# Gaps in front of four groups of SBUF buffers, so that the operands of the split products start at one address modulo 512 bytes

## The chip, the cores and the metric

One core of a Trainium2 chip runs the whole program in one launch. The metric is device time in microseconds (us), the median of several executions.

## The reference

512 tokens of width 1024 pass through two blocks in float32. The first has two layers, each a mix of two attentions, a mixture of experts and a gated embedding. The second has one layer: windowed attention, a linear recurrence, block attention, and a dense gated feed-forward. Cut to its matrix products:

```python
def first_block(x, ...):
    for i in range(2):
        u = rmsnorm(x, g_mix[i]) @ w_in[i]
        y_a = stick_breaking_attention(...) @ w_br_a[i]
        y_b = differential_attention(...) @ w_br_b[i]
        merged = sigmoid(gate_a) * y_a + sigmoid(gate_b) * y_b
        x = x + merged @ w_o[i]
        x = x + hierarchical_moe(rmsnorm(x, g_ffn[i]), ...)
        x = x + (p[i] @ w_ple[i]) * sigmoid(rmsnorm(x, g_ple[i]) @ w_ple_gate[i])
    return rmsnorm(x, g_final)

def hybrid_layer(x, ...):
    z = rms_norm(x, g_mix) @ w_in
    merged = gt[:, :, 0] * (o_a @ p_a) + gt[:, :, 1] * (o_b @ p_b) + gt[:, :, 2] * (o_c @ p_c)
    x = x + merged @ w_out
    gate, up = jnp.split(rms_norm(x, g_ffn) @ w_gu, 2, axis=-1)
    return x + (jax.nn.silu(gate) * up) @ w_down
```

## The kernel before, in words

All activations stay in SBUF, tokens or features on the 128 partitions. Nearly every dense product is a **split product** (`split_product`, line 134, its matmul is line 137): both operands are held as a high and a low part of type float32r, and three matmuls add high x high, high x low and low x high into one PSUM bank:

```python
for n, (left, right) in enumerate(((a[0], b[0]), (a[0], b[1]), (a[1], b[0]))):
    last = nc.tensor.matmul(out, left, right, start=(start and n == 0), stop=(stop and n == 2), ...)
```

`left` is the stationary operand, 128 columns that TensorE loads first; `right` is the moving one, 512 columns. The profile names them in the order moving, stationary: `banks<-h_split,w_high` moves h_split over w_high.

Weights come through a `Stream` (line 143): SyncE issues the load of a 512 KB piece into one of four raw buffers, GpSimd casts it to the high part (line 178), VectorE subtracts for the low part (line 189), and TensorE uses one of three split buffers. `columns` (line 195) moves the 512 tokens of the normalised activations `h_split` over a weight chunk, eight chunks of three matmuls for a piece; `rows` moves weights over tokens. `Merge` (line 1179) computes for each of eight output chunks the branch products (`ya`, `yb`, in the second block also `yc`, moving, over the stream's weights) and the gates (`columns`, two per chunk in the first block, done early inside the attention for three of the eight chunks; three per chunk in the second). `Product` (line 1290) moves weights over `op_split`, the split form of the merged activations: 24 matmuls for each of eight chunks, and for each of 22 hidden chunks in the second block's down product. The gate product of the embedding has its own stream, `pg`. In the attentions, `columns` and `rows` of later pieces stand between the attention's own matmuls.

The order of the work is written out by hand for each engine (the `sync`, `gpsimd`, `tensor`, `scalar` and `vector` functions), with semaphores between them.

**Where buffers lie.** Memory is a stack in each partition: a buffer starts where the last one ended, rounded up to 32 bytes. `region` (with `h_split` over its first part) is placed by `Core`. The first block's large buffers share one space, the ring, that begins at `ring_base` (in `program`): the stream `w1`, `ya_transposed`, `yb_transposed`, `op_split` are placed in it by `Opening`, as are later `expert_ring`, `ex_xs`, `ex_xsT` and `pg_high`. Expert weights take six slots in turn, four in the ring and two in the region. The second block's stream `w2` begins where `first_stack` began, and `yb2_transposed`, `yc2_transposed` and `op2_split` follow the window attention's buffers. Both blocks' buffers appear in the profile without the block's number (`w_high`, `yb_transposed`, `op_split`).

Of the kernel before, what the change touches and what calls it, by code (L numbers as in the profile page):

```python
# [21 lines left out]
F32 = mybir.dt.float32  # L22
# [7 lines left out]
P = 128  # L30
# [6 lines left out]
NEG = -1e30  # L37
HD = 64
SCALE = HD ** -0.5


class Core:


    def __init__(self, nc, ctx):
        def sb(name, shape, dt=F32):
            return ctx.enter_context(nc.sbuf_tensor(name, shape, dt))

        self.nc = nc
        self.used_sems = set()  # L50
        self.ps = ctx.enter_context(nc.psum_tensor("banks", [P, 8, 512], F32))
        self.x = sb("x_tokens", [P, NT, D])
        self.ident = sb("identity", [P, P])
        self.ident_r = sb("identity_r", [P, P], F32R)
        self.neg_tri = sb("neg_tri", [P, P], F32R)
        self.neg_ones = sb("neg_ones", [P, P], F32R)
        self.neg_before = sb("neg_before", [P, P], F32R)
        self.strict_bias = sb("strict_bias", [P, P], F32R)
        self.chunk_bias = sb("chunk_bias", [P, P], F32R)
        self.rope_swap = sb("rope_swap", [P, P])  # L60
        self.shift = sb("shift", [P, 16])
        self.halves = sb("halves", [P, 2, 2, NT])
        self.norm_ss, self.norm_g = sb("norm_ss", [P, 2, NT]), sb("norm_g", [P, 2, DC])
        self.layer = ""
        offset = nc.sbuf_base
        assert offset % 32 == 0
        self.region = sb("region", [P, 3 * NT * D])
        self.h = nc.alloc_sbuf_tensor_at("h_split", [P, 2, DC, S], F32R, offset=offset)
        self.spare = self.region[:, 2 * NT * D:]
        self.spare_tiles = self.spare.rearrange("p (t d) -> p t d", t=NT)  # L70

    def room(self, ctx, name, shape, dt=F32):
        return ctx.enter_context(self.nc.sbuf_tensor(name + self.layer, shape, dt))
# [152 lines left out]
def row_piece(w, c, chunks, off, cols):  # L226

    return [(chunks, cols, rows_pc(w)[:, c:c + chunks, off:off + cols])]
# [291 lines left out]
def stick_breaking(k, ctx, room, norm, st, yT, da_raw):  # L520
# [114 lines left out]
    def scalar(act):  # L635
        def take_q(i, bank):
            pair = (i - SB_COLUMNS) // 2
            act.wait_ge(st.used, i + 1)
            dst = qT[:, pair % 2, :] if pair < pairs else da_raw[:, 0, :]
            nc.scalar.activation(dst, k.ps[:, bank, :], ACT.Copy, scale=SCALE).then_inc(q_ready, 1)  # L640

# [191 lines left out]
def differential(k, ctx, room, st, lams, gain, lam_init, keep, cosT, sinT, raw, yT, early, line_store=None):  # L833
# [139 lines left out]
    def scalar(act):  # L973
        def take_raw(head, n, bank):
            act.wait_ge(st.used, columns_of(head, n) + 1)
            nc.scalar.activation(raw[:, n, :], k.ps[:, bank, :], ACT.Copy,
                                 scale=1.0 if n else SCALE).then_inc(sem["raw_ready"], 1)

# [1112 lines left out]
def window_attention(k, ctx, room, norm, st, bias, first_bias, yT, conv, rooms_free):  # L2091
# [172 lines left out]
    def scalar(act):  # L2264
        def take_q(i, bank):
# [3 lines left out]
            if g:  # L2269
                src, dst = src.rearrange("p (i r) -> p r i", r=APART), dst.rearrange("p (r i) -> p r i", r=APART)  # L2270
            nc.scalar.activation(dst, src, ACT.Copy, scale=SCALE).then_inc(q_ready, 1)

# [199 lines left out]
def block_attention(k, st, lines, bias, first_bias, yT, opened):  # L2472
# [11 lines left out]
    with ExitStack() as ctx:  # L2484
# [90 lines left out]
        def _(act):  # L2575
# [14 lines left out]
            def take_q(i):  # L2590
                act.wait_ge(st.used, i + 1)
                nc.scalar.activation(qT[:, (i - QK) // 2 % 2, :], k.ps[:, 7, :], ACT.Copy, scale=SCALE).then_inc(q_ready, 1)

# [473 lines left out]
def second_layer(k, t, lines, out, ple_of, ending, ring_base):  # L3067
    nc = k.nc
    ended = set(k.used_sems)
    w_in = t["w_in_2"][0]  # L3070
    width = WINDOW_HEADS * HD
    window = len(WINDOW_GROUPS) * width
    lru, block = 3 * window, 3 * window + 1024
    gates = block + 1536
    packs = (0, 1), (2,)
    with ExitStack() as mix:
        st = Stream(k, mix, "w2", [row_piece(w_in, 4 * e, 4, 2 * window, width) for e in (0, 1)]
                    + [column_piece(w_in, 2 * window + g * width + pair * P) for g in (1, 2) for pair in (0, 1)]
                    + [column_piece(w_in, kind * window + g * width + pair * P) for pair in (0, 1)
                       for g in range(len(WINDOW_GROUPS)) for kind in (0, 1)]  # L3080
                    + [column_piece(w_in, lru + c * P) for c in range(8)]
                    + [row_piece(w_in, 2 * e, 2, block + 1024, 512) for e in range(4)]
                    + [column_piece(w_in, block + kind * 512 + pair * P) for pair in range(4) for kind in (0, 1)]
                    + merge_pieces(w_in, (gates, gates + D, gates + 2 * D), (t["p_a_2"][0], t["p_b_2"][0], t["p_c_2"][0]),
                                   packs)
                    + [[(1, D, t["w_out_2"][0][c * P:(c + 1) * P, :].rearrange("p (a n) -> p a n", a=1))] for c in range(DC)]
                    + [column_piece(t["w_gu_2"][0], part * FFN + f * P) for f in range(FC) for part in (0, 1)]
                    + [[(1, D, t["w_down_2"][0][f * P:(f + 1) * P, :].rearrange("p (a n) -> p a n", a=1))] for f in range(FC)])
        mix_base = nc.sbuf_base
        yaT = mix.enter_context(nc.sbuf_tensor("ya2_transposed", [P, 2, 2, S], F32R))  # L3090
        bias = mix.enter_context(nc.sbuf_tensor("biases", [P, 4, S], F32))
        conv = Convolution(k, mix, t["conv_w_2"][0], t["conv_b_2"][0], t["lru_ba_2"][0], t["lru_bx_2"][0], t["lru_lam_2"][0])
        window_bias_loads, block_bias_loads = window_bias(k, mix, bias, lines), block_bias(k, mix, bias, lines)
        with ExitStack() as room:
            junk = nc.alloc_sbuf_tensor_at("fn_junk", [P, NT * D], F32, offset=ring_base + 4 * 18432)[:]
            closing_g = nc.alloc_sbuf_tensor_at("fn_g", [P, D], F32, offset=ring_base + 4 * 26624)[:]
            sig = nc.alloc_sbuf_tensor_at("pe_sig", [P, 4, 512], F32, offset=ring_base + 4 * 27648)[:]
            xn = nc.alloc_sbuf_tensor_at("mix2_xn", [P, NT, D], F32, offset=ring_base + 4 * 22528)[:]
            norm = FinalNorm(k, mix, "mix2", t["g_mix_2"][0], (6, 7), xn, junk, t["g_final"], k.spare_tiles, closing_g)
            moe, ple, gate_stream = ple_of(mix, norm, sig, junk, st)  # L3100
            attention = window_attention(k, mix, room, norm, st, bias, window_bias_loads, yaT, conv, (gate_stream.used, 2 * NT))

            def sync(sp):
                norm.load_closing(sp)
                ple[0](sp)

            border(k, moe, (sync, *ple[1:]), attention)
        ending.close()
        ybT = mix.enter_context(nc.sbuf_tensor("yb2_transposed", [P, 2, 4, S], F32R))
        qkv_base = nc.sbuf_base  # L3110
        block_qkv = mix.enter_context(nc.sbuf_tensor("ba_qkv", [P, 8, S], F32))
        opened = (block_qkv[:, 0:2, :], block_qkv[:, 2:4, :], block_qkv[:, 4:8, :])
        recurrence(k, st, (18, 26, 30), conv, t["lru_wa_2"][0], t["lru_wx_2"][0], ybT, block_bias_loads, opened, ended)
        k.used_sems -= ended


        assert S // 256 - 1 <= 3
        ycT = mix.enter_context(nc.sbuf_tensor("yc2_transposed", [P, 2, 4, S], F32R))
        block_attention(k, st, lines, bias, block_bias_loads, ycT, opened)
        mergedT = k.spare.rearrange("p (c s) -> p c s", c=DC)  # L3120
        split = nc.alloc_sbuf_tensor_at("op2_split", [P, 2, 2, S], F32R, offset=qkv_base)
        silu = nc.alloc_sbuf_tensor_at("ff_silu", [P, 2, S], F32, offset=qkv_base + 4 * 4 * S)
        final_g = nc.alloc_sbuf_tensor_at("final_g", [P, D], F32, offset=qkv_base + 4 * 6 * S)
        hiddenT = nc.alloc_sbuf_tensor_at("ff_hiddenT", [P, FC, S], F32, offset=mix_base)
        assert mix_base + 4 * FC * S <= qkv_base
        sig, part = (mix.enter_context(nc.sbuf_tensor("mg2_" + n, [P, 2, S], F32)) for n in ("sig", "part"))
        m = Merge(k, mix, "mg2", st, 38, packs, ((yaT, 2), (ybT, 4), (ycT, 4)), mergedT, sig, part)
        op = Product(k, mix, "op2", st, m.end, DC, mergedT, split)
        fd = Product(k, mix, "fd", st, m.end + DC + 2 * FC, FC, hiddenT, split)
        second_half(k, st, m, op, fd, t["g_ffn_2"][0], t["g_final_2"], hiddenT, silu, final_g, out)  # L3130
# [39 lines left out]
def first_layer(k, t, i, ctx, ending, r, ring_base, scratch, o, line_store):  # L3170


    nc = k.nc
# [12 lines left out]
            line_store)  # L3186
    o.branches.close()
    k.used_sems -= ended
    assert -(-nc.sbuf_base // 32) * 32 == ring_base
    mergedT = k.spare.rearrange("p (c s) -> p c s", c=DC)  # L3190
    m = Merge(k, ctx, "mg", st, MERGE_PIECES, o.packs, ((o.yaT, 4), (o.ybT, 4)), mergedT, o.sig, o.part,
              (0, 1, 2, 3, 4, 7, 5, 6), early, early_ready)
# [41 lines left out]
def program(nc, t, out):  # L3234
    with ExitStack() as ctx:
        k = Core(nc, ctx)
# [4 lines left out]
        first_stack = ctx.enter_context(ExitStack())  # L3241
# [6 lines left out]
        xn_rows = nc.dram_tensor("xn_rows", [S, D], F32)  # L3248
        y_rows = nc.dram_tensor("y_rows", [2 * S, D], F32)
        r = Routing(nc, first_stack)  # L3250
        ring_base = -(-nc.sbuf_base // 32) * 32
        ple = None
        layers = [ctx.enter_context(ExitStack()) for _ in range(DEPTH)]
        endings = [ctx.enter_context(ExitStack()) for _ in range(DEPTH)]
# [111 lines left out]
```

## Time and profile before

| | us |
|---|---|
| median of three runs | 2525.43 |
| the three runs | 2525.5, 2521.73, 2525.43 |
| span of the profiled execution, first to last instruction | 2525.1 |
| TensorE busy (11776 matmuls) | 2315.6 |
| VectorE, ScalarE, GpSimd busy | 1001.0, 585.6, 410.2 |

No own device time stands beside the profiled execution other than its span; the median of the runs is 0.3 above it. In the profile TensorE's matmuls are pipelined: each is shown with a duration of about 390 ns, while the next begins after some 230 ns. So what a matmul takes in a long train is read from the start of one to the start of another, divided by the number between, and not from its duration. A row of the timeline merges neighbours of a kind (x2), and of the three matmuls of a split product the one with the low weights stands alone.

### The profile page before, as it was taken

How to read it: one execution, taken by the hardware profiler on the slowest of the kernel's cores; microseconds unless marked ns; L12 is line 12 of the kernel's file. 1: busy time of each engine (PE TensorE's matmuls, PEld its weight loads, DVE VectorE, ACT ScalarE, POOL GpSimd, SP SyncE). 2: the span in 40 equal slices, each digit the busy share in tenths (PEclk: the TensorE clock that was granted, in tenths of full speed). 3: DMA queues.
4: the chain of work that ended last, by engine and by line, in shares of the span. 5: the costliest groups of instructions: out<-in, count | busy, mean ns of one | idle time of the engine just before them, and what ended most of it. 6: DMA issues, size and time to landing. Idle time of an engine off the chain costs nothing. (4 is left out here: it accounts for less than half of the span.)

```text
span 2525.1 us, 29142 instructions
## 1 busy us (share of the span) xinstructions
PE 2315.6 (92%) x11776; PEld 1707.1 (68%) x11776; DVE 1001.0 (40%) x1730; ACT 585.6 (23%) x1211; POOL 410.2 (16%) x404
## 2 busy tenths in 40 slices
PE   7989999588889999999778988899999999999998
PEld 5766788444447766688644545787767887888886
DVE  5445533511135354543521114545653334322234
ACT  2433401211123352321301113423442001100011
POOL 2011121112211101111111211111111221111111
PEclk9999999799998999999989999899999999999999
DMA  4114535699982212232779995222322333233321
GB/s 147 51 44 102 133 106 203 235 410 415 415 332 67 67 34 61 64 89 89 305 306 416 415 398 190 68 84 68 88 76 71 93 103 101 84 99 94 100 92 67
DMA packets 291540, 402.85 MB, mean 160 GB/s; under 512 B 31306, under 2 KB 230730, under 8 KB 273478
## 3 DMA queue, kind: packets, MB, share of 16 engines
q1 hardware_dynamic: 276444, 373.31, 42.0%
q0 software_dynamic: 10176, 16.81, 1.8%
q10 hardware_dynamic: 4778, 10.76, 1.6%
q8 instruction: 98, 1.61, 0.3%
q14 instruction: 44, 0.36, 0.0%
HBM read 388.99 MB, written 30.15 MB: 166 GB/s over the span
## 5 line engine op out<-in xcount | busy, mean ns | idle before, releaser
L137 PE MATMUL banks<-h_split,w_high 128*128 128x512 f32 x2624 | 829.4, 397 | 2.7 <-PEq L3035 1.7
L137 PEld LDWEIGHTS banks<-h_split,w_high 128*128 128x128 f32 x2624 | 481.5, 188 | 107.9 <-issue 8.2
L189 DVE TENSOR_TENSOR w_low<-w_raw,w_high 128x1024 fp32r<-128x1024 f32 (+1 forms) x264 | 316.9, 1201 | 526.6 <-POOL w_high L178 526.5
L178 POOL CAST w_high<-w_raw 128x1024 fp32r<-128x1024 f32 (+1 forms) x264 | 278.2, 1055 | 1475.1 <-PE banks L137 1352.2
L137 PE MATMUL banks<-h_split,w_low 128*128 128x512 f32 x1312 | 514.6, 392 | 0.0
L137 PEld LDWEIGHTS banks<-h_split,w_low 128*128 128x128 f32 x1312 | 246.5, 188 | 55.0
L137 PE MATMUL banks<-w_high,op_split 128*128 128x512 f32 x736 | 231.3, 394 | 1.0 <-DVE mg_part L1269 1.0
L1839 PE MATMUL banks<-expert_ring,ex_xsT 128*64 128x256 f32 x1472 | 180.2, 400 | 17.3 <-DMA expert_ring<-in_w_exp_up 14.3
L137 PEld LDWEIGHTS banks<-w_high,op_split 128*128 128x128 f32 x736 | 138.2, 188 | 34.0 <-DVE mg_part L1269 2.2
L1839 PEld LDWEIGHTS banks<-expert_ring,ex_xsT 128*64 128x64 f32 x1472 | 107.5, 144 | 75.7 <-DMA expert_ring<-in_w_exp_up 15.5
L137 PE MATMUL banks<-w_low,op_split 128*128 128x512 f32 x368 | 144.7, 393 | 0.0
L1798 POOL DMA_INDIRECT y_rows<-ex_y,route_row x66 | 65.8, 997 | 394.7 <-ACT ex_y L1882 394.7
L1910 DVE TENSOR_TENSOR ex_hid<-ex_silu,banks 128x128 f32<-128x128 f32 x66 | 19.0, 288 | 269.7 <-ACT ex_silu L1887 269.7
L137 PE MATMUL banks<-w_high,h_split 128*128 128x512 f32 (+1 forms) x384 | 121.4, 391 | 2.7 <-DVE h_split L337 2.5
L1253 ACT ACTIVATE mg_sig<-banks 128x512 f32<-128x512 f32 x44 | 26.3, 598 | 347.3 <-PE banks L137 347.3
L1828 PE MATMUL banks<-identity,ex_xs 128*128 128x128 f32 x272 | 44.1, 311 | 64.1 <-DMA ex_xs<-xn_rows,route_token 41.2
L1857 PE MATMUL banks<-expert_ring,ex_hidT 128*64 128x512 f32 x368 | 94.9, 639 | 0.9 <-issue 0.9
L1828 PEld LDWEIGHTS banks<-identity,ex_xs 128*128 128x128 f32 x272 | 36.0, 198 | 78.4 <-DMA ex_xs<-xn_rows,route_token 52.1
L137 PE MATMUL banks<-pg_high,h_split 128*128 128x512 f32 x256 | 86.2, 412 | 2.3 <-issue 2.3
L137 PEld LDWEIGHTS banks<-w_high,h_split 128*128 128x128 f32 x384 | 73.0, 195 | 18.3 <-DVE h_split L337 3.7
L1882 ACT ACTIVATE ex_y<-banks 128x512 f32<-128x512 f32 x66 | 39.4, 598 | 187.7 <-PE banks L1857 187.7
L137 PEld LDWEIGHTS banks<-w_low,op_split 128*128 128x128 f32 x368 | 69.1, 188 | 15.9
(424 smaller groups left out, 2768.6 us busy)
## 6 DMA issues: line engine op xcount, KB each, us to landing
w_raw<-in_w_in SPq DMA_DIRECT2D x142, 512.0 KB, 4.1
expert_ring<-in_w_exp_gate SPq DMA_DIRECT2D x46, 1024.0 KB
expert_ring<-in_w_exp_up SPq DMA_DIRECT2D x46, 1024.0 KB
expert_ring<-in_w_exp_down SPq DMA_DIRECT2D x46, 1024.0 KB
w_raw<-in_w_gu SPq DMA_DIRECT2D x44, 512.0 KB, 4.1
region<-in_w_exp_gate SPq DMA_DIRECT2D x20, 1024.0 KB
region<-in_w_exp_up SPq DMA_DIRECT2D x20, 1024.0 KB
region<-in_w_exp_down SPq DMA_DIRECT2D x20, 1024.0 KB
```

Source lines behind the costliest of these rows:

```text
L137: last = nc.tensor.matmul(out, left, right, start=(start and n == 0), stop=(stop and n == 2), skip_group_check=True)
L178: self.nc.gpsimd.tensor_copy(self.high[:, i % self.SPLIT, 0:n], self.raw[:, i % self.RAW, 0:n]).then_inc(self.high_ready, 1)
L189: self.nc.vector.tensor_tensor(self.low[:, i % self.SPLIT, 0:n], self.raw[:, i % self.RAW, 0:n], self.high[:, i % self.SPLIT, 0:n].bitcast ...
L1253: self.nc.scalar.activation(out, gate, ACT.Sigmoid).then_inc(self.sig_done, 1)
L1798: nc.gpsimd.indirect_dma_start(out=y_halves, in_=y[:, n % Y, :], in_offset=None, out_offset=bass.IndirectOffsetOnAxis(ap=r.row[:, at:at + ...
L1828: last = nc.tensor.transpose(k.ps[:, c // 4, (c % 4) * P:(c % 4 + 1) * P], xs[:, q % X, c::DC], k.ident[:])
L1839: last = nc.tensor.matmul(k.ps[LANES * h:LANES * (h + 1), 2 + side, 0:2 * P].rearrange("p (g n) -> p g n", g=2), xsT[:, q % X, c, LANES * ...
L1857: last = nc.tensor.matmul(k.ps[LANES * h:LANES * (h + 1), 5 + n % 2, :], hidT[:, n % 2, LANES * f:LANES * (f + 1)], slots[n % U][1][:, f, ...
L1882: nc.scalar.activation(y[:, n % Y, :], k.ps[:, 5 + n % 2, :], ACT.Copy).then_inc(sem["y_ready"], 1)
L1910: nc.vector.tensor_tensor(hid[:, n % 2, :], silu[:, n % 2, :], k.ps[:, 2 + n % 2, P:2 * P], ALU.mult).then_inc(sem["hid_ready"], 1)
```

## The change

`aligned` allocates an unused gap such that the next buffer starts at a multiple of 512 bytes. It is called at four places: before `region`, before the ring, before the second block's stream, and before `yb2_transposed`.

```diff
+LINE_BYTES = 512
...
-        offset = nc.sbuf_base
-        assert offset % 32 == 0
+        offset = self.aligned(ctx, "region")
         self.region = sb("region", [P, 3 * NT * D])
...
+    def aligned(self, ctx, name):
+        gap = -(-(-self.nc.sbuf_base // 32) * 32) % LINE_BYTES
+        if gap:
+            ctx.enter_context(self.nc.sbuf_tensor(name + "_gap", [P, gap // 4], F32))
+        assert self.nc.sbuf_base % LINE_BYTES == 0
+        return self.nc.sbuf_base
...
     with ExitStack() as mix:
+        k.aligned(mix, "w2")
         st = Stream(k, mix, "w2", [row_piece(w_in, 4 * e, 4, 2 * window, width) for e in (0, 1)]
...
         ending.close()
+        k.aligned(mix, "yb2")
         ybT = mix.enter_context(nc.sbuf_tensor("yb2_transposed", [P, 2, 4, S], F32R))
...
-    assert -(-nc.sbuf_base // 32) * 32 == ring_base
+    assert nc.sbuf_base == ring_base
...
-        ring_base = -(-nc.sbuf_base // 32) * 32
+        ring_base = k.aligned(first_stack, "ring")
```

The addresses in a partition that the allocation gives, before and after, in bytes, and their rest modulo 512:

| buffer | before | rest | after | rest |
|---|---|---|---|---|
| identity | 32896 | 128 | 32896 | 128 |
| region, h_split | 37216 | 352 | 37376 | 0 |
| route_w_high | 94624 | 416 | 94784 | 64 |
| ring, ya_transposed | 99008 | 192 | 99328 | 0 |
| yb_transposed | 115392 | 192 | 115712 | 0 |
| pg_high | 148160 | 192 | 148480 | 0 |
| da_diff | 156352 | 192 | 156672 | 0 |
| w1_raw | 172736 | 192 | 173056 | 0 |
| w1_high | 189120 | 192 | 189440 | 0 |
| ex_xs | 197312 | 192 | 197632 | 0 |
| op_split | 213696 | 192 | 214016 | 0 |
| w2_raw | 88928 | 352 | 89088 | 0 |
| w2_high | 105312 | 352 | 105472 | 0 |
| ya2_transposed | 129888 | 352 | 130048 | 0 |
| wa_probs | 199808 | 128 | 199968 | 288 |
| yb2_transposed | 162944 | 128 | 163328 | 0 |
| yc2_transposed | 195712 | 128 | 196096 | 0 |
| op2_split | 179328 | 128 | 179712 | 0 |
| ba_probs | 212096 | 128 | 212480 | 0 |

A low part lies a multiple of 4096 bytes behind its high part. The instructions of every engine and their order are the same as before.

## Rows read from the trace of the kernel before

**Rows 1.** The page, busy time of each engine (us, share of the span, instructions)
```profile
PE 2315.6 (92%) x11776; PEld 1707.1 (68%) x11776; DVE 1001.0 (40%) x1730; ACT 585.6 (23%) x1211; POOL 410.2 (16%) x404
```

**Rows 2.** Windows: us from start, length, TensorE busy (matmuls), granted clock, DMA share, GB/s
```profile
25.00:300.00 275.00, 263.30 (x1301) 1.00 0.33 85
325.00:390.00 65.00, 65.00 (x281) 1.00 0.34 103
505.00:720.00 215.00, 188.63 (x1303) 0.96 1.02 413
735.00:800.00 65.00, 60.92 (x237) 0.95 0.38 139
2150.00:2390.00 240.00, 239.03 (x1061) 1.00 0.32 95
```

**Rows 3.** Waits of TensorE: line <- what ended it: us in total, times, longest
```profile
PE banks L1828 <- DMA ex_xs<-xn_rows,route_token: 41.2, 24, 3.4
...
PE banks L1839 <- DMA expert_ring<-in_w_exp_up: 14.3, 6, 3.7
...
PE banks L581 <- issue: 5.0, 6, 0.8
...
PE banks L137 <- DVE h_split L337: 4.5, 5, 1.5
...
PE banks L596 <- DVE sb_stay L721: 3.5, 2, 1.7
```

**Rows 4.** The chain that ended last: start us, us, what
```profile
2154.13 361.26 PE banks L137 x1578
```

**Rows 5.** Timeline of TensorE, feed-forward of the second block: start us, us, instruction
```profile
2200.03 0.39 PE L137 MATMUL banks<-h_split,w_low 128*128 128x512 f32 x1
...
2209.55 0.39 PE L137 MATMUL banks<-h_split,w_low 128*128 128x512 f32 x1
```

**Rows 6.** Timeline of TensorE, merge of the second block
```profile
1926.19 0.61 PE L137 MATMUL banks<-h_split,w_high 128*128 128x512 f32 x2
...
1933.67 0.61 PE L137 MATMUL banks<-ya_transposed,w_high 128*128 128x512 f32 x2
...
1935.03 0.63 PE L137 MATMUL banks<-yb_transposed,w_high 128*128 128x512 f32 x2
...
1939.23 0.63 PE L137 MATMUL banks<-yc_transposed,w_high 128*128 128x512 f32 x2
```

**Rows 7.** Timeline of TensorE, merge of the first layer
```profile
323.81 0.63 PE L137 MATMUL banks<-h_split,w_high 128*128 128x512 f32 x2
...
335.05 0.63 PE L137 MATMUL banks<-ya_transposed,w_high 128*128 128x512 f32 x2
...
337.81 0.61 PE L137 MATMUL banks<-yb_transposed,w_high 128*128 128x512 f32 x2
...
340.53 0.63 PE L137 MATMUL banks<-h_split,w_high 128*128 128x512 f32 x2
```

**Rows 8.** Timeline of TensorE, down product of the second block
```profile
2409.98 0.63 PE L137 MATMUL banks<-w_high,op_split 128*128 128x512 f32 x2
...
2419.78 0.40 PE L137 MATMUL banks<-w_high,op_split 128*128 128x512 f32 x1
```

**Rows 9.** Matmul groups of 25 to 1620 us, then of 1620 to 2525: xcount | busy us, mean ns
```profile
L137 PE MATMUL banks<-h_split,w_high 128*128 128x512 f32 x1024 | 332.8, 406 | 0.0
...
L137 PE MATMUL banks<-pg_high,h_split 128*128 128x512 f32 x256 | 86.2, 412 | 2.3 <-issue 2.3
...
L137 PE MATMUL banks<-w_high,op_split 128*128 128x512 f32 x480 | 151.4, 396 | 0.3 <-DVE mg_part L1269 0.3
```

**Rows 10.** Timeline of TensorE, attention of the second block
```profile
1841.81 0.40 PE L137 MATMUL banks<-h_split,w_low 128*128 128x512 f32 x1
...
1843.89 0.40 PE L137 MATMUL banks<-h_split,w_low 128*128 128x512 f32 x1
```

**Rows 11.** DMA issues of 860 to 1180 us: xcount, KB each, median us to landing
```profile
w_raw<-in_w_in SPq DMA_DIRECT2D x27, 512.0 KB, 3.9
```

**Rows 12.** DMA issues of 1900 to 2100 us
```profile
w_raw<-in_w_in SPq DMA_DIRECT2D x21, 512.0 KB, 4.2
```

## The prediction

> **What bounds the kernel now.** I began with busy time. TensorE is busy for 2315.6 of the 2525.1 us, no other engine for more than 1001.0 [rows 1], so what one matmul takes decides. Next the stages: over 263.3 of 275.0 us in the first layer's attention, 65.0 of 65.0 in its merge, 239.03 of 240.0 in the feed-forward, TensorE works; only in the expert stage (188.63 of 215.0) do the DMA engines run full, at a share of 1.02 and 413 GB/s [rows 2]. The list of waits says who holds TensorE up: first the gathered rows and the expert weights (41.2 and 14.3 us); in the attentions the longest entry is 5.0 us, in six pieces, and for L137, the line of the split products, the longest is 4.5 [rows 3]. The chain that ended last is this line too: 361 us of it in one unbroken piece up to 2515 us [rows 4]. So a nanosecond off each matmul of L137 comes off the end nearly everywhere.
>
> Then the timeline of TensorE, read as start to start. A split product is three matmuls of 512 columns, high, low, high, so a "low" row comes once in three.
> - Feed-forward, moving h_split (352 past a multiple of 512), stationary w2 (352): from 2200.03 to 2209.55 us are 42 matmuls, **226.7 ns** each [rows 5].
> - The second block's merge. Gates, again h_split and w2: from 1926.19 to 1933.67 are 33, 226.7 each. Then yb2 and yc2 (both 128) with the same w2: from 1935.03 to 1939.23 are 18, **233.3** each [rows 6].
> - The first layer's merge. h_split (352) with w1 (192): 323.81 to 335.05 are 48, **234.2** each. Then ya and yb (both 192) with w1: 335.05 to 337.81 are 12 at 230, 337.81 to 340.53 are 12 at **226.7** [rows 7].
> - The second block's down product, w2 (352) with op_split (128): 2409.98 to 2419.78 are 42 at 233.3 [rows 8].
>
> Within one stage, at a full clock, under the same transfers, the slow operand is h_split in one block and yb in the other. What goes with it in every case is whether the moving and the stationary operand start at the same address modulo 512 bytes: equal 226.7, unequal 233.3 to 234.2.
>
> **The rule against it.** The Trainium skill (TensorE: Matmul & The Clock Gate, "Step-by-step: what each phase is for") gives TensorE two independent SBUF read ports and says that loading the next tile's weights "doesn't steal SBUF read bandwidth from the running matmul"; by that rule two operands can't disturb each other wherever they lie, and the change would give nothing: 2525. The trace disagrees: 6.6 to 7.5 ns per matmul between operands that differ in address alone. The page's 215.7 ns for back-to-back matmuls isn't reached in either case; I sum with the rows.
>
> **The change part by part.** No instruction is added, removed or moved on any engine, and no wait. The three gaps (160 bytes before the region, 160 before the ring, 224 before yb2; none is needed before w2, which lands on a multiple of 512 by the first gap) cost space and no time. What changes is the pairing, at 226.7 instead of:
> 1. Second block's two products (out product 8 chunks x 24 matmuls, down product 22 x 24, together 720, the 480 with w_high and half as many with w_low [rows 9]): 6.6 ns each, **4.8 us**. TensorE is never idle there but for the norm between them.
> 2. yb2 and yc2 in the merge, 8 chunks x 24 = 192 matmuls, 6.6 ns: **1.3 us**.
> 3. First block's merges: five chunks x two gates x 24 x two layers are 480 matmuls at 7.5 ns, 3.6 us; the ya matmuls behind them, 120 at 230, settle no more: 0.4. **4.0 us**.
> 4. Embedding's gate product, 256 + 128 = 384 matmuls of pg with h_split [rows 9], the pairing 192 with 352. Its stage has a granted clock of 0.95 [rows 2], so I count 350 at 6.6, less a settling at the start: **2.1 us**.
> 5. First block's attentions: of 1024 + 512 column matmuls [rows 9] 1056 are left, and four trains of 96 row matmuls (w moving, 384). The row matmuls come in long trains: some 350 at full clock x 6.6 is 2.3, of which I take 2.1. The column ones stand in trains of five to eleven between attention steps, and such trains don't reach 226.7 even with equal addresses: in the second block's attention 1841.81 to 1843.89 are 9 at 231 [rows 10]. I give the first block's the 234 of [rows 7]. So 3 ns each, not 7, for some 950 that follow another one closely: 2.9. **5.0 us**.
> 6. Nothing: pairs that are equal already (h_split with w2, ya and yb with w1, w1 with op_split), and the router's product (64 apart before and after). Cost: the identity matrix stays at 128, while da_diff, ba_probs, wa_probs, ex_xs move from 192 or 128 to 0 or 288. The 60 and 80 transposes of wa_probs and ba_probs lose their match. The trace has no price for a mismatch at 128 columns; bounds are 0 and the 7 ns of a matmul four times as long, so 0 to 1 us. I take 0.2, nearer to the quarter of 7. What mismatched before (da_diff, ex_xs) stays so.
> 7. Transfers now land at multiples of 512. Bounds from the landings of 512 KB pieces: 3.9 us at offset 192 in the second layer [rows 11], 4.2 at 352 in the second block [rows 12]: either sign, within some 7%. They lie under matmuls except in the expert stages. I take 0 and keep both signs as rivals.
>
> Sum 4.8 + 1.3 + 4.0 + 2.1 + 5.0 - 0.2 = **17.0 us** off the profiled span of 2525.1, so 2508.1. The median of the runs, 2525.43, lies 0.3 above that span, so 2508.4. **What is late next:** in the attentions, DVE and ScalarE run beside TensorE, and where it now waits a little (1.7 us at most at a time for sb_stay [rows 3]) it will wait longer by what it gains. If all of part 5 went that way, 12 us would be left. In the expert stages the transfers' start moves up with TensorE, since the slots come free by its first results, so the earlier gain isn't lost there. If nothing settled and each mismatched matmul gained 7 ns, it would be 22 us.
>
> **Rivals.**
> - *Nothing happens.* The pairing was another one than modulo 512 (by a larger power of two, say), or zero is itself a bad offset. For: no operand of before starts at 0, so that residue isn't shown. Against: equal offsets give 226.7 both at 192 and at 352, and w2 minus h_split is an odd multiple of 512, so neither the value nor 1024 matters. Time 2525, chance 0.07.
> - *Slower: the expert weights land slower at offset 0.* Place: the expert stage of each layer, 215 us at 413 GB/s with the DMA share at 1.02 [rows 2], so 430 us. There a change of 5% of the transfers is 21.5 us. For: 3.9 against 4.2 shows that offset and landing may go together. Against: the lists compare different neighbours, and expert slots in the region (352) and in the ring (192) alternate in one stream. It decides at 4%, where it eats the 17 us; at 5.2% the kernel is 5 us slower, 2530. Chance 0.03.
> - *Faster still: the same mechanism with the other sign.* At 5% 2487. An expert packet is 8 KB or 4 KB where those of w_raw are 512 bytes, and if the cost hangs on a packet's start, a sixteenth of 5% of 430 us is 1.3 us. Between those, 2% is 9 us: 2499. Chance 0.05. The Trainium skill (DMA: Bandwidth & Descriptors, "How a descriptor splits into AXI transactions") says that a descriptor that doesn't start at a multiple of 256 bytes pays unused beats, one per 32 bytes: for 192, 6 on 256 of an 8 KB packet, 2.3%, 10 us of 430. It would make the buffer at 192 slower than that at 352 (3 beats); the landings are the other way round.
> - *Absorbed:* attention gives nothing and part of the rest is lost to waits, 8 us left, 2517. Chance 0.05.
>
> **How the numbers follow.** The forecast holds the remaining 0.80, with its own range from 12 to 22 us off, 2503 to 2513; the three runs of before spread over 3.8 us, so I widen it by 2 or 3 on each side: 2500 to 2515, which also touches the small form of the DMA rivals. A measurement of this kernel tells about 0.2%, 5 us. Faster by more: 0.80 + 0.05 + 0.05 = 0.90; within: 0.07; slower: 0.03.
>
> **What would show it.** In the profile after: the low rows of every long train 0.68 us apart, also for yb, yc, op_split in the second block and h_split with w1 and pg; short trains at 229 to 231; second block's down product of 528 matmuls shorter by 3.5 us; expert stage still at 412 GB/s. If the trains stay at 233 ns anywhere among these, the reading of the addresses is wrong. If they all drop and the span doesn't by over 10 us, the list of waits must show new ones in the attentions or experts.

## The result, and the profile after

The changed kernel takes **2500.68 us** in the median of four runs (2498.89 to 2501.39), the kernel before 2524.61 beside it on the same chip (four runs, 2521.73 to 2525.5): a ratio of **0.9909, interval 0.9896 to 0.9922**. It is 23.9 us faster; forecast were 2508.4 us, 17.0 off, in a range of 2500 to 2515. The span of the profiled execution fell from 2525.1 to 2499.2, by 25.9.

In the windows of the profile after, the columns are those of [rows 2]: us from start, length and TensorE's busy time (matmuls), granted clock, DMA share, GB/s.

```profile
25.00:300.00 275.00, 263.20 (x1312) 1.00 0.32 85
325.00:390.00 65.00, 65.00 (x288) 1.00 0.34 106
505.00:720.00 215.00, 184.33 (x1315) 0.99 1.01 417
735.00:800.00 65.00, 56.33 (x240) 0.97 0.37 131
2150.00:2390.00 240.00, 240.00 (x1060) 1.00 0.32 97
```

In the attention, the merge and the feed-forward TensorE is as busy as it was, and the merge holds more matmuls in its 65 us. The line to notice is the third: the expert stage moves 417 GB/s where it moved 413. The granted clock of that line is 0.99 where it was 0.96, so by itself it doesn't tell whether transfers or the clock made the difference. From the page and the chain of waits of the profile after, the lines that answer to [rows 1] and [rows 4]:

```profile
PE 2287.3 (92%) x11776; PEld 1700.3 (68%) x11776; DVE 1002.5 (40%) x1730; ACT 585.6 (23%) x1211; POOL 408.8 (16%) x404
...
2131.75 357.71 PE banks L144 x1578
```

TensorE has 28.3 us less to do by the page's modelled durations, the other engines the same. The chain's last piece, the second block's feed-forward with its down product, is 3.55 us shorter; the prediction named 3.5 for the down product.

The timeline of TensorE after, start us, us, instruction. Line numbers are 7 higher than before, so the split product is L144. First the first layer's merge (of before [rows 7]), then the second block's merge [rows 6], its down product [rows 8], and a short train in its attention [rows 10]:

```profile
321.78 0.61 PE L144 MATMUL banks<-h_split,w_high 128*128 128x512 f32 x2
...
332.66 0.61 PE L144 MATMUL banks<-ya_transposed,w_high 128*128 128x512 f32 x2
...
335.38 0.61 PE L144 MATMUL banks<-yb_transposed,w_high 128*128 128x512 f32 x2
...
1915.34 0.62 PE L144 MATMUL banks<-yb_transposed,w_high 128*128 128x512 f32 x2
...
1920.10 0.62 PE L144 MATMUL banks<-yc_transposed,w_high 128*128 128x512 f32 x2
...
2384.34 0.62 PE L144 MATMUL banks<-w_high,op_split 128*128 128x512 f32 x2
...
2393.86 0.39 PE L144 MATMUL banks<-w_high,op_split 128*128 128x512 f32 x1
...
1822.27 0.40 PE L144 MATMUL banks<-h_split,w_low 128*128 128x512 f32 x1
...
1824.35 0.40 PE L144 MATMUL banks<-h_split,w_low 128*128 128x512 f32 x1
```

h_split with w1 now takes 10.88 us for 48 matmuls, 226.7 ns each (was 234.2); the ya matmuls behind them 2.72 for 12, again 226.7 and no settling (was 230); from the first yb row to the last yc row are 21 in 4.76, 226.7 (was 233.3); the down product has 42 in 9.52, 226.7 (was 233.3). The short train, equal before and after, still takes 2.08 for 9, 231 ns.

The matmul records of each kernel give the same as one sum: for every split-product matmul of 512 columns that the next one follows after 220 to 245 ns, what it takes above 226.7. Below this is called the **excess**. It is 22.35 us before and 4.88 after, 17.5 us less. So the pairing gave what was forecast of it, and some 6 to 8 us came from elsewhere.

To find where, take the start of the same TensorE instruction in both profiles: how much earlier it comes, split by stage.

| TensorE, from | until | gained, us |
|---|---|---|
| start | first layer's router (463.7 us before) | 4.0 |
| there | first expert matmul (489.3) | -0.5 |
| there | last expert matmul (734.9) | **5.1** |
| there | second layer's router (1254.1) | 8.0 |
| there | first expert matmul (1279.2) | -0.3 |
| there | last expert matmul (1526.7) | **2.7** |
| there | window attention (1685.7) | 0.6 |
| there | end | 6.3 |

The expert stages have none of the split products counted in the excess (no interval in them falls under its rule), and yet 7.8 us come from them. They are the stages in which transfers set the pace [rows 2]. (One profile against one: how far such a table scatters comes below.) From the waits of TensorE after (of before [rows 3]; line <- what ended it: us, times, longest):

```profile
PE banks L1835 <- DMA ex_xs<-xn_rows,route_token: 29.9, 22, 2.5
...
PE banks L1846 <- DMA expert_ring<-in_w_exp_up: 21.4, 11, 3.4
...
PE banks L1846 <- DMA region<-in_w_exp_up: 7.7, 3, 3.6
```

They are 59.0 us in all and were 58.9, so the list shows no gain: it tells that TensorE still waits for transfers, not how fast these are. The page's line on the DMA queue that carries the weights does (packets, MB, share of 16 engines in the span), before and after:

```profile
q1 hardware_dynamic: 276444, 373.31, 42.0%
```

```profile
q1 hardware_dynamic: 276444, 373.31, 41.7%
```

The same packets and bytes take 42.0% of 2525.1 us, 1061 us of each engine, and then 41.7% of 2499.2, 1042: 1.7% less. From the single records, with the mean over the expert slots' packets of 8 KB while the stream runs steadily: 314.8 ns in the ring and 315.0 in the region before, 309.8 and 309.7 after. That is 1.65%, and 1.65% of the two stages' 430 us is 7.1 us. Two things changed at once for these transfers and the matmuls beside them, so the rest is for experiments.

### The profile page after: what moved, and what is told of

The parts are those of the page before. It is cut to its first block and busy times, and to the rows that moved or that the text cites. A ratio compares the mean times of both kernels' runs of the same rounds, so it can differ in the third digit from the quotient of the medians.

```text
span 2499.2 us, 29142 instructions
## 1 busy us (share of the span) xinstructions
PE 2287.3 (92%) x11776; PEld 1700.3 (68%) x11776; DVE 1002.5 (40%) x1730; ACT 585.6 (23%) x1211; POOL 408.8 (16%) x404
## 3 DMA queue, kind: packets, MB, share of 16 engines
q1 hardware_dynamic: 276444, 373.31, 41.7%
## 5 line engine op out<-in xcount | busy, mean ns | idle before, releaser
L144 PE MATMUL banks<-h_split,w_high 128*128 128x512 f32 x2624 | 824.5, 395 | 2.8 <-PEq L3042 1.7
L144 PEld LDWEIGHTS banks<-h_split,w_high 128*128 128x128 f32 x2624 | 481.0, 188 | 104.4 <-issue 8.2
L144 PE MATMUL banks<-h_split,w_low 128*128 128x512 f32 x1312 | 512.0, 390 | 0.0
L144 PEld LDWEIGHTS banks<-h_split,w_low 128*128 128x128 f32 x1312 | 246.3, 188 | 52.7
L144 PE MATMUL banks<-w_high,op_split 128*128 128x512 f32 x736 | 228.2, 390 | 1.1 <-DVE mg_part L1276 1.1
L144 PEld LDWEIGHTS banks<-w_high,op_split 128*128 128x128 f32 x736 | 138.1, 188 | 31.2 <-DVE mg_part L1276 2.4
L144 PE MATMUL banks<-w_low,op_split 128*128 128x512 f32 x368 | 143.2, 389 | 0.0
L144 PE MATMUL banks<-w_high,h_split 128*128 128x512 f32 (+1 forms) x384 | 119.4, 386 | 3.0 <-DVE h_split L344 2.8
L144 PE MATMUL banks<-pg_high,h_split 128*128 128x512 f32 x256 | 84.2, 404 | 2.6 <-issue 2.6
L144 PEld LDWEIGHTS banks<-w_high,h_split 128*128 128x128 f32 x384 | 72.4, 193 | 17.1 <-DVE h_split L344 3.8
L1846 PE MATMUL banks<-region,ex_xsT 128*64 128x256 f32 x640 | 75.0, 388 | 7.7 <-DMA region<-in_w_exp_up 7.7
L1894 ACT ACTIVATE ex_silu<-banks 128x128 f32<-128x128 f32 x66 | 18.3, 278 | 270.4 <-PE banks L1846 270.4
```

The source lines that it names most:

```text
L1846: last = nc.tensor.matmul(k.ps[LANES * h:LANES * (h + 1), 2 + side, 0:2 * P].rearrange("p (g n) -> p g n", g=2), xsT[:, q % X, c, LANES * ...
L1894: nc.scalar.activation(silu[:, n % 2, :], k.ps[:, 2 + n % 2, 0:P], ACT.Silu).then_inc(sem["silu_done"], 1)
```

## The experiments

Theories: **P**, the pairing alone, 17 us. **L**, in addition the expert transfers land faster at multiples of some power of two, 7 us. Seven of the ten kernels give `aligned` a table of rests in place of the zero, and that table is the whole difference between them:

```diff
+RESTS = {"region": 0, "ring": 0, "w2": 0, "yb2": 0}
...
-        gap = -(-(-self.nc.sbuf_base // 32) * 32) % LINE_BYTES
+        rest = RESTS[name]
+        gap = (rest - -(-self.nc.sbuf_base // 32) * 32) % LINE_BYTES
...
-        assert self.nc.sbuf_base % LINE_BYTES == 0
+        assert self.nc.sbuf_base % LINE_BYTES == rest
```

With four zeros this is the changed kernel. In what follows four numbers are the rests of region, ring, w2 and yb2. Lines are 2 higher again: the split product is L146.

### All pairs equal, but at 352

```diff
+RESTS = {"region": 352, "ring": 352, "w2": 352, "yb2": 352}
```

> All four groups start 352 past a multiple of 512, none at a multiple: every split pair is equal again, but no transfer lands at a multiple of 256. Theory P+L (pairing gives about 17.5 us, landings at a multiple of 256 give the other 6 or 7): long trains at 226.7 ns everywhere, expert stage at 413 GB/s as before, 8 KB packets at 314 ns, about 2507 us. Rival Z (the offset zero itself does it, for TensorE too): trains of h_split with w1 at 233 to 234 ns, 2524 us. Rival N (the extra 6 or 7 us come from TensorE's trains or from the clock, not from landings): as the change, 2501 us.

Measured: 2506.85 us, ratio 0.9933 (0.992 to 0.9945) to before. The timeline has the first merge as in the changed kernel, 48 matmuls in 10.88 us:

```profile
321.21 0.62 PE L146 MATMUL banks<-h_split,w_high 128*128 128x512 f32 x2
...
332.09 0.62 PE L146 MATMUL banks<-ya_transposed,w_high 128*128 128x512 f32 x2
```

The excess is 4.85. But packets take 314.4 and 314.9 ns, as before. The pairing alone gives its 17 us (2525.3 in the median of before less 2506.85 is 18.5), and it does so at a common rest of 352 as at zero; the other 6 us are gone with the zero.

### Landings at multiples of 256, pairs apart

```diff
+RESTS = {"region": 0, "ring": 256, "w2": 0, "yb2": 128}
```

> Region and second stream at 0, ring at 256, yb2 group at 128: every expert transfer lands at a multiple of 256, but h_split and w1 are 256 apart and w2 and yb2 are 128 apart. Theory P+L: trains at 233 ns in the first block, and of yb, yc and op_split in the second; expert stage at 420 GB/s or more, packets at 310; about 2518 us. If the pairing counts modulo 256 and not 512, the first block's trains fall to 226.7 and the time to about 2507. Rival N: no gain, 2524.

Measured: 2507.35 us, ratio 0.9925 (0.9912 to 0.9938). Packets take 309.8 ns, so a landing at 256 is as good as at 0. The surprise is in the matmuls. First merge, where h_split and w1 are 256 apart, then down product, w2 and op_split 128 apart:

```profile
321.19 0.62 PE L146 MATMUL banks<-h_split,w_high 128*128 128x512 f32 x2
...
332.07 0.62 PE L146 MATMUL banks<-ya_transposed,w_high 128*128 128x512 f32 x2
...
2390.12 0.62 PE L146 MATMUL banks<-w_high,op_split 128*128 128x512 f32 x2
...
2399.88 0.40 PE L146 MATMUL banks<-w_high,op_split 128*128 128x512 f32 x1
```

48 in 10.88 is 226.7: **operands 256 apart don't disturb each other**. 42 in 9.76 is 232.4: at 128 they do. The pairing goes by 256 bytes and not by 512, as the prediction had it. So the first block gains here and the second doesn't; the excess is 10.30, 12.05 less than before. In all 18.0 us were gained by the medians (2525.3 less 2507.35) and 18.9 by the ratio. What lies between, 6 to 7 us, is what the landings give.

The expert stages of the two runs, from 560 to 690 and from 1340 to 1480 us. All at 352:

```profile
560.00:690.00 130.00, 112.61 (x790) 0.97 1.02 416
1340.00:1480.00 140.00, 122.21 (x827) 0.95 1.02 416
```

Landings at 0 and 256:

```profile
560.00:690.00 130.00, 113.11 (x792) 0.97 1.02 422
1340.00:1480.00 140.00, 126.93 (x867) 0.95 1.02 422
```

At the same granted clock and the same full DMA share, 416 against 422 GB/s. Before it is 415, in the changed kernel 422.

### The second block alone

In the kernel before, one gap ahead of yb2, so that yb2, yc2 and op2_split start at 352 like w2:

```diff
         ending.close()
+        gap = (nc.sbuf_base // 512 * 512 + 512 + 352 - nc.sbuf_base) % 512
+        mix.enter_context(nc.sbuf_tensor("yb2_gap", [P, gap // 4], F32))
+        assert nc.sbuf_base % 512 == 352
```

> The kernel before with one gap alone, before yb2, which brings yb2, yc2 and op2_split to 352, the offset of w2. Theory P: 912 matmuls go from 233.3 to 226.7 ns, 6.0 us off, 2518.6; nothing else moves. Rival Z (zero itself is what counts): no gain, 2524.6.

Measured: 2519.06 us, ratio 0.9975 (0.9964 to 0.9985), 6.2 us off. Its second merge, yb with w2 and then yc (lines as before, since nothing ahead of them moved):

```profile
1931.38 0.62 PE L137 MATMUL banks<-yb_transposed,w_high 128*128 128x512 f32 x2
...
1934.10 0.62 PE L137 MATMUL banks<-yc_transposed,w_high 128*128 128x512 f32 x2
...
1935.46 0.62 PE L137 MATMUL banks<-yc_transposed,w_high 128*128 128x512 f32 x2
```

18 in 4.08 is 226.7. The excess falls by 6.4, to 15.95. This confirms parts 1 and 2 of the sum (4.8 + 1.3) with one gap of 224 bytes and nothing else.

### The constants too

Is there more to be had where pairs are still unequal, or in the short trains? This kernel gives `x_tokens`, the router's weights and the window attention's buffers a rest of zero too, by moving the small constants and one gap:

```diff
+        self.shift = sb("shift", [P, 16])
+        self.halves = sb("halves", [P, 2, 2, NT])
+        self.norm_ss, self.norm_g = sb("norm_ss", [P, 2, NT]), sb("norm_g", [P, 2, DC])
+        self.aligned(ctx, "x")
...
+        self.w_high, self.w_low = (sb(n, [P, self.W + 96], F32R) for n in ("w_high", "w_low"))
...
+    k.aligned(room, "wa")
```

> The change, and x_tokens, the identities and masks, the router's weights and the window attention's buffers at multiples of 512 too. If the slow starts of the short trains (234, 232, 232, 230 ns ...) come from transposes and masks whose operands lie 128 apart from the rest, they vanish: up to 3 or 4 us more, 2497. If they come from the narrow matmuls themselves, only the router's 48 matmuls gain, 0.3 us: 2500.5.

Measured: 2501.83 us, ratio 0.9921 (0.989 to 0.9952): no gain over the change. (One of the six runs took 2526.12 us, at a granted clock of 0.965 where the others have 0.970 to 0.972; it makes the interval wide.) The short train is where it was, 9 matmuls in 2.08 us:

```profile
1821.53 0.40 PE L145 MATMUL banks<-h_split,w_low 128*128 128x512 f32 x1
...
1823.61 0.39 PE L145 MATMUL banks<-h_split,w_low 128*128 128x512 f32 x1
```

The excess is 4.29, against 4.88 and 4.79 in the two profiles of the change. So nearly all that is left of it doesn't come from the alignment of these buffers. By place in its train, a matmul is followed after about 232 ns at the start, and after 226.7 behind the first ten or so.

### Other distances, other landings

Distances and landings that are neither equal nor at 256. First ring and yb2 at a distance of 64 and 32, then of 128 and 480:

```diff
+RESTS = {"region": 0, "ring": 64, "w2": 0, "yb2": 32}
```

> Region and second stream at 0, ring at 64, yb2 group at 32: h_split and w1 64 apart, w2 and yb2 32 apart, and in one stream of expert loads four slots begin at 64 and two at a multiple of 256. Theory 256 (operands are in step when their starts agree modulo 256, and any other distance costs the same 7 ns): trains at 233 to 234 ns in the first block, 233 in the second's yb, yc and op_split. If the distance sets the size, 64 and 32 give something between 226.7 and 233. Landings: flat theory (any start off a multiple of 256 costs a packet of 8 KB 5 ns) 314.5 ns into the ring, 309.7 into the region; by wasted beats (two of 256 at 64) 312 into the ring. Time about 2520.

```diff
+RESTS = {"region": 0, "ring": 128, "w2": 0, "yb2": 480}
```

> Region and second stream at 0, ring at 128, yb2 group at 480. Theory 256: trains at 233 to 234 ns with 128 between h_split and w1, 233 with 480 between w2 and yb2; packets into the ring 314.5 ns, into the region 309.7; about 2520 us. If 128 is enough for either, first block's trains at 226.7 (then about 2508), or packets into the ring at 309.7.

Measured: 2517.1 us, ratio 0.9972 (0.9962 to 0.9982), and 2518.23, ratio 0.9976 (0.9965 to 0.9986). The first merge with the ring at 64:

```profile
323.24 0.63 PE L146 MATMUL banks<-h_split,w_high 128*128 128x512 f32 x2
...
334.44 0.62 PE L146 MATMUL banks<-ya_transposed,w_high 128*128 128x512 f32 x2
```

The same with the ring at 128:

```profile
323.04 0.62 PE L146 MATMUL banks<-h_split,w_high 128*128 128x512 f32 x2
...
334.23 0.63 PE L146 MATMUL banks<-ya_transposed,w_high 128*128 128x512 f32 x2
```

11.20 and 11.19 us for 48, 233.3 and 233.1. Pairs at 32 and at 480 take 233.3 to 233.6 in the second block, and the excess is 18.48 and 19.89. It is nearly all or nothing, with one exception. In the embedding's gate product of the run with 64, pg moves at 64 over h_split at 0, the roles of the merge reversed:

```profile
770.24 0.62 PE L146 MATMUL banks<-pg_high,h_split 128*128 128x512 f32 x2
...
775.74 0.62 PE L146 MATMUL banks<-pg_high,h_split 128*128 128x512 f32 x2
```

24 in 5.50 is 229.2, less than half of the loss. The row matmuls of the first block's attentions, w1 at 64 moving over h_split, show the same in their excess: it is 0.9 us where it was 2.4. The packets of the ring take 312.9 ns at 64 and 312.3 at 128, between the two values so far, and the stages run at 418 and 419 GB/s.

### The ring at 256

```diff
+RESTS = {"region": 0, "ring": 256, "w2": 0, "yb2": 0}
```

> The change with the ring 256 bytes further: h_split and w1 are 256 apart, all else as in the change. Theory 256: no difference from the change, trains at 226.7 to 228.7 ns, packets 309.7 ns, 2500.7 us. If 512 counts after all, 11 us longer, 2512.

Measured: 2502.73 us, ratio 0.9916 (0.9901 to 0.9931), span 2499.8. Trains at 226.7 (excess 4.68), packets at 309.6 to 310 ns, 422 GB/s: all as in the change, though h_split now lies 256 from w1 and from pg. So 256 is enough for both effects. The intervals of this kernel and of the change overlap: no difference between them is shown.

### The change, 352 and 32, once more on one chip

The difference of 6 us between rests of zero and 352 rested on measurements apart from each other. So the change, all at 352 (the kernel of the first experiment) and all at 32 were run side by side:

> The changed kernel, on the same chip as the next two: 2500.7 us, expert stage at 422 GB/s.

> All four groups at 352 once more, beside the change on the same chip. Pairing is equal in both, so what lies between them is the landings alone: packets of 8 KB at 314.5 against 309.7 ns, 416 against 422 GB/s, and 6 us of time (2506.8). If landings give nothing, both show the same time.

```diff
+RESTS = {"region": 32, "ring": 32, "w2": 32, "yb2": 32}
```

> All four groups at 32: pairing equal, landings 32 past a multiple of 256. TensorE's trains as in the change, 226.7 ns. By the beats that a late start wastes (one of 256), packets take 311 ns and the time is 2502; if any start off a multiple of 64 costs the same as 352 does, 314.5 ns, 416 GB/s and 2506.8.

| kernel | us | ratio to before | excess | 8 KB packet, ns | GB/s |
|---|---|---|---|---|---|
| change | 2503.85 | 0.9917 (0.9903 to 0.993) | 4.79 | 309.7 | 422 |
| all 352 | 2510.99 | 0.9936 (0.9922 to 0.9949) | 4.94 | 314.5 to 315 | 415, 416 |
| all 32 | 2510.99 | 0.9944 (0.9931 to 0.9958) | 4.76 | 315.1 to 315.8 | 415 |

The two that land off a multiple of 256 are both 7.1 us above the change in the median, 6.0 and 7.1 in the mean of their five runs. The ratios' intervals still touch that of the change, so the times alone make the difference likely and its size uncertain by some 3 us; that it comes from the transfers is what the packets and the GB/s show. The same kernel at 352 took 2506.85 the first time and 2510.99 now, 18.5 and 14.6 below the kernel before beside it: that is how far such a difference can be trusted. The windows show the transfers once more. All at 352:

```profile
560.00:690.00 130.00, 112.51 (x784) 0.97 1.02 416
1340.00:1480.00 140.00, 120.88 (x851) 0.98 1.02 415
```

All at 32:

```profile
560.00:690.00 130.00, 117.18 (x810) 0.96 1.02 415
1340.00:1480.00 140.00, 120.23 (x841) 0.98 1.02 415
```

The change:

```profile
560.00:690.00 130.00, 115.08 (x810) 0.97 1.02 422
1340.00:1480.00 140.00, 119.00 (x827) 0.96 1.02 422
```

And in the table by stage (same TensorE instruction against the one profile of the kernel before), the two expert stages give 8.8 us in this run of the change, 7.8 in the first, 7.2 and 7.1 with the ring at 256 and with the constants moved, and 6.0 with landings at 0 and 256; they give 3.4, 1.3 and 0.8 in the three runs that land at 352 or 32. The gap in the second block alone gives 3.9 there, though nothing of these stages changed in it. So a single entry is uncertain by some 4 us; the means of the two groups lie 5 us apart, and some 2 us of the first table's 7.8 are chance of the one profile before.

## Why the prediction was right, and where not

**What bounds it, and the pairing: right.** Long trains between operands that start alike take 226.7 ns and others 232 to 234, now shown in both directions: kernels with equal pairs and landings that are off a multiple of 256 gained 18.5, 14.6 and 14.6 us (17.4 to 17.6 by the excess), and one gap in the second block alone gained 6.2. By the steps of the sum, in us:

| step | forecast | measured |
|---|---|---|
| 1, second block's products | 4.8 | 4.7 |
| 2, yb2 and yc2 | 1.3 | 1.3 |
| 3, first block's merges | 4.0 | 3.9 |
| 4, embedding's gate product | 2.1 | 1.9 to 2.1 |
| 5, first block's attentions | 5.0 | 5.2 |
| 6, transposes | -0.2 | 0, nothing seen |
| 7, landings | 0 | about +6 |

The measured ones of 1 to 5 are the falls of the excess in each part. Short trains gained some 4 ns a matmul, more than half of a long one's 6.6, where step 5 took 3 from [rows 10]; the row trains gained 1.8 us, where it took 2.1. The two errors partly cancel. The times fell by about what the excess did, so no large part was lost to waits for DVE or ScalarE, and "absorbed" is out.

**Step 6.** The transposes with ba_probs lose their match with identity (128 and 128, now 128 and 0). Of before and of after, all instructions of that line (median, mean and longest ns by duration, from when to when):

```profile
L2544 PE MATMUL banks<-identity,ba_probs x80: 270/272/473, 1837.1 to 1905.6; 128*128 128x128 f32 x80
```

```profile
L2551 PE MATMUL banks<-identity,ba_probs x80: 270/273/473, 1817.5 to 1886.1; 128*128 128x128 f32 x80
```

They start 109 ns apart in the median in both, and so do those of wa_probs. A mismatch costs nothing measurable at 128 columns here; the scaling by a quarter was wrong, by little.

**The modulus.** "The same address modulo 512" was too narrow: 256 apart is as good as equal. No pair of before was 256 apart, so the rows could not tell, and the sum didn't depend on it.

**The step that failed is 7, "I take 0".** The landings gained about 6 us: 6.2 between the change and all at 352 as first measured, 7.1 (6.0 by the means) with both run side by side, 6 to 7 left over in the run with landings alone, 5 by the expert stages. By the packets it would be 7.1 (1.65% of 430 us), an estimate that takes the whole of both stages as paced by transfers. That brought 2508.4 down to 2500.7, to the edge of the range. The gain, 23.9 us, lies outside the forecast's own 12 to 22; that the time is inside is owed to the 2 or 3 us by which the range was widened for the spread of the runs. The prediction notes that this touches the small form of the DMA rivals, but gave that form no place in the sum: for the lower edge to hold was in part luck. The sign "expert stage still at 412 GB/s" failed too: it moves 417 in the same window, and 422 in its steady part. What the landings gave is the rival "faster still", which had 0.05, in its small form: its 2% and 2499 us were nearly what happened. Two arguments had made it small. The first was the landing of 512 KB pieces, 3.9 us at 192 against 4.2 at 352 [rows 11, 12]. After the change the lists of DMA issues show both of these at a multiple of 512, of 840 to 1160 and of 1880 to 2080 us:

```profile
w_raw<-in_w_in SPq DMA_DIRECT2D x28, 512.0 KB, 3.8
```

```profile
w_raw<-in_w_in SPq DMA_DIRECT2D x21, 512.0 KB, 3.9
```

The one at 352 gained 0.3 and the one at 192 gained 0.1, both in the good direction; read as "either sign" in the prediction, they had compared two offsets that are both bad, and none that is good. The second was the scaling by a packet's start, a sixteenth of the loss, 1.3 us. It took the small difference between those lists as the whole price, and it took the cost as one per packet. The expert stages hold packets of two sizes, and these say otherwise: from 560 to 690 us the 8 KB packets fell by 5.2 ns (315.0 to 309.8) and the 4 KB packets by 2.8 (161.8 to 159.0), the same 1.7% of each. The cost goes with the bytes and not with the number of starts. The loss itself could not be read from the trace of before, since the ring's packets (at 192) and the region's (at 352) take the same 315 ns there; so the honest chance of this rival was larger than 0.05.

The Trainium skill (DMA: Bandwidth & Descriptors, "How a descriptor splits into AXI transactions"), weighed in the prediction, is right in sign and rough size for the 8 KB packets: an unaligned start costs unused beats. For a start at 192 an estimate by it gives 2.3%, where 1.6% was measured. In how the cost goes with the offset the measurement decides otherwise. By the page's rule a rest of 32 modulo 256 costs one beat and one of 192 six, whatever the packet's size, which would be twice the share of a 4 KB packet; here the 4 KB packet loses the same share, and the 8 KB packet takes 309.7 ns at 0, 315.1 to 315.8 at 32, 312.9 at 64, 314.9 at 96 (352), 312.3 at 128 and 314.8 at 192. Rests that are multiples of 64 but not 192 cost about half, the others all of it. The other rule that the prediction weighed, two independent read ports for TensorE (the Trainium skill, TensorE: Matmul & The Clock Gate, "Step-by-step: what each phase is for"), doesn't lead to the time here: what was drawn from it, that operands can't disturb each other wherever they lie, is contradicted by each run that changes their distance (226.7 against 232.4 to 234.2 ns). Whether the ports themselves are the place, no run shows.

**Left open.** What in the memory makes unequal operands slow: no run looked inside it. Why 64 with reversed roles costs 2.5 ns and not 6.6. Whether the effect is the same for other types and widths than float32r at 512 columns. Why 32 costs a packet more than 64. In single executions the granted clock differs (0.968 in the mean before, 0.973 after), and by stage they scatter by 2 to 4 us; so the 2 or 3 us between the two effects (17.5 and about 6) and the 25.9 of the spans aren't assigned to anything. No kernel tried is shown to be faster than the change.

## What to carry to other kernels

Where long trains of matmuls bound a kernel, read start to start per pair of operands and set it against their addresses; 7 ns of 234 for a few hundred bytes of padding is a good bargain, and it was found by comparing pairs in one stage under one clock. Give both operands and every buffer that transfers fill a start at a multiple of 256 bytes; when a table of addresses holds no good case of a thing, don't price that thing at zero. And where a stage is paced by transfers, look at the packets' time and the GB/s there, since the waits by name didn't show the gain.

## What the runs showed of the hardware that was not expected

- Moving and stationary operand of a 512-column float32r matmul, by their distance modulo 256: 0 gives 226.7 ns; 32, 128, 160, 224, and 64 in one role give 232.4 to 234.2; 64 in the other role 229.2. The common rest doesn't matter (0, 32, 192, 352).
- An 8 KB packet landing in SBUF takes 309.7 ns at a multiple of 256, 312.3 to 312.9 at 64 and 128, 314.4 to 315.8 at 32, 96 and 192. A 4 KB packet takes 159.0 to 159.4 at a multiple of 256 and 161.7 to 162.3 at 32, 96 and 192. At a DMA share of 1.02 that is 422, 418 to 419, and 415 to 416 GB/s.
- Transposes of 128 columns (109 ns start to start) show no such effect, and short trains of 512-column matmuls start at about 232 ns even with equal operands.
